# Expert rooms by rank in 53 units, the next layer's adaLN inside the attention, and TensorE weighing two of eight choices

## What is computed

```python
def _trunk_layer(x, mod, layer_idx, p, ctx=None):
    sh1, sc1, g1, sh2, sc2, g2 = jnp.split(mod[:, None, :], 6, axis=-1)
    h = _rmsnorm(x, p['norm_g'][0]) * (1 + sc1) + sh1
    proj = h @ p['w_in']
    ...
    mix = jnp.concatenate([fn_out, a, hg_out], axis=-1) @ p['w_out']
    x = x + g1 * mix
    h2 = _rmsnorm(x, p['norm_g'][1]) * (1 + sc2) + sh2
    x = x + g2 * _moe(h2.reshape(b * l, D_MODEL), p).reshape(b, l, D_MODEL)

def _moe(h, p):
    scores = jax.nn.sigmoid((h @ p['w_router']).astype(jnp.float32))
    ...
    _, eidx = lax.top_k(jnp.where(emask, biased, -jnp.inf), TOP_K)
    w = jnp.take_along_axis(scores, eidx, axis=1)
    w = w / jnp.sum(w, axis=-1, keepdims=True) * ROUTED_SCALE
    gates = jnp.sum(jax.nn.one_hot(eidx, N_EXPERTS, dtype=jnp.float32) * w[..., None], axis=1)
    hg = jnp.einsum('td,edf->tef', h, p['w_gate'])
    hu = jnp.einsum('td,edf->tef', h, p['w_up'])
    act = jax.nn.silu(hg) * hu * gates[:, :, None].astype(h.dtype)
    routed = jnp.einsum('tef,efd->td', act, p['w_down'])
    shared = (jax.nn.silu(h @ p['ws_gate']) * (h @ p['ws_up'])) @ p['ws_down']
    return routed + shared

# mod of layer l: jax.nn.silu(c) @ w_ada[l] + b_ada[l]   (6 x 1024 values; c_ctx for the prompt)
```

## Time and profile before

| | |
|---|---|
| median of 3 runs | 1691.47 us (1687.89 to 1701.95) |
| the profiled execution | 1706.42 us, span 1704.6 us |
| TensorE busy in the span | 1406.1 us (82%) |
| DVE, ACT, POOL busy | 671.4, 408.3 and 256.3 us |
| mean granted TensorE clock | 0.881 of full speed |
| chain that ended last | TensorE 71%, DVE 16%, DMA 6%, issue 4% |

### The profile page before, as it was taken

How to read it: one execution, slowest core, us unless ns; L and a number is a source line. 1 busy time by engine, 2 the same in 40 slices (tenths; PEclk the granted TensorE clock), 3 DMA queues, 4 the chain that set the end, 5 groups by cost and what they waited for, 6 DMA issues and landing times.

```text
span 1704.6 us, 23713 instructions
## 1 busy us (share of the span) xinstructions
PE 1406.1 (82%) x8772; PEld 962.6 (56%) x8772; DVE 671.4 (39%) x1382; ACT 408.3 (24%) x788; POOL 256.3 (15%) x273
## 2 busy tenths in 40 slices
PE   4799687986999999997059996888889999999942
PEld 2598465954555555554028875676655555555521
DVE  4422767153332222222743347633523222222246
ACT  2324425021222222221013344321112122222201
POOL 1000000001322222231010000000023232322200
PEclk9799857977999999999579996699889999999975
DMA  9553202126988888885874412122469888888853
GB/s 319 206 183 118 105 31 109 50 87 233 362 305 317 328 333 324 305 332 181 340 257 173 141 70 99 41 99 99 180 252 358 333 313 307 324 294 298 328 207 154
DMA packets 126098, 378.96 MB, mean 222 GB/s; under 512 B 28224, under 2 KB 33152, under 8 KB 122784
## 3 DMA queue, kind: packets, MB, share of 16 engines
q1 hardware_dynamic: 86976, 291.31, 46.2%
q0 software_dynamic: 35552, 60.97, 10.1%
q10 hardware_dynamic: 3456, 25.17, 3.6%
HBM read 480.36 MB, written 64.75 MB: 320 GB/s over the span
## 4 chain that ended last, share of the span: by engine, by line
PE 71%; DVE 16%; DMA 6%; issue 4%; ACT 2%; SPq 0%; DVEq 0%; ACTq 0%; POOLq 0%
PE bank L1143 25%; PE bank L1158 11%; PE bank L1129 7%; PE bank L1050 5%; PE bank L771 4%; PE bank L772 4%; PE bank L773 4%; DVE aT L1843 4%; DMA ring<-in_w_ada 3%; DVE aT L1580 1%; PE bank L1066 1%; DMA ring<-in_w_in 1%; PE bank L790 1%; PE bank L1114 1%; PE bank L976 1%
## 5 line engine op out<-in xcount | busy, mean ns | idle before, releaser
L1143 PE MATMUL bank<-slab,xT 128*64 128x256 f32 x2112 | 301.5, 396 | 20.6 <-issue 20.5
L1143 PEld LDWEIGHTS bank<-slab,xT 128*64 128x64 f32 x2112 | 180.6, 142 | 104.2 <-issue 38.2
L732 POOL DMA_INDIRECT sums_scratch<-h,row_table x112 | 112.8, 1007 | 538.6 <-PE bank L1129 438.4
L1826 DVE TENSOR_TENSOR work<-work,bank 128x128 f32<-128x128 f32 x112 | 32.3, 288 | 399.1 <-ACT work L1405 399.1
L1143 PE MATMUL bank<-ring,xT 128*64 128x256 f32 x960 | 152.7, 392 | 9.6 <-issue 9.6
L1158 PE MATMUL bank<-slab,work 128*64 128x512 f32 x528 | 147.3, 592 | 1.5 <-DVE work L1832 1.5
L1405 ACT ACTIVATE work<-bank 128x128 f32<-128x128 f32 x112 | 31.1, 278 | 457.5 <-PE bank L1143 457.5
L1815 DVE COPY h<-bank 128x512 f32<-128x512 f32 x112 | 77.5, 692 | 127.0 <-PE bank L1158 127.0
L1143 PEld LDWEIGHTS bank<-ring,xT 128*64 128x64 f32 x960 | 90.1, 140 | 44.8 <-issue 14.8
L1143 PE MATMUL bank<-h_hi_slot,xT 128*64 128x256 f32 x512 | 108.5, 396 | 6.4 <-issue 6.4
L1492 DVE TENSOR_TENSOR w_lo<-ring,w_hi 128x2048 fp32r<-128x2048 f32 x24 | 55.0, 2292 | 122.3 <-ACT w_hi L1229 122.3
(11 more groups left out here) (334 smaller groups left out, 2324.9 us busy)
## 6 DMA issues: line engine op xcount, KB each, us to landing
slab<-in_w_gate SPq DMA_DIRECT2D x112, 512.0 KB
slab<-in_w_up SPq DMA_DIRECT2D x112, 512.0 KB
slab<-in_w_down SPq DMA_DIRECT2D x112, 512.0 KB
ring<-in_w_ada SPq DMA_DIRECT2D x24, 2048.0 KB
ring<-in_w_gate SPq DMA_DIRECT2D x52, 512.0 KB
ring<-in_w_up SPq DMA_DIRECT2D x52, 512.0 KB
ring<-in_w_down SPq DMA_DIRECT2D x52, 512.0 KB
slab<-sums_scratch ACTq DMA_DIRECT2D x24, 1024.0 KB, 11.5
```

Source lines behind the costliest of these rows:

```text
L732: pool.indirect_dma_start(sums_dram, bass.IndirectOffsetOnAxis(ap=row_table[:, u:u + 1], axis=0), y_rows[:, n % 3, :], None, bounds_check= ...
L1143: last = mm(bk[r, 0:2 * P].rearrange("p (k f) -> p k f", k=2), xT[:, n % 2, j, r], w[:, j, :, :], start=(j == 0), stop=(j == NJ - 1))
```

## The change

- Rooms by rank. `windows_of` gives each unit its tiles: ranks 0 to 7 have 128 rows each, now as one tile of 128 columns ("whole", 8 units); ranks 8 to 15 have 96 rows and share their unit with a rank of 56 to 63, which has 32 rows ("mixed", 8 units, tiles 0:64, 64:96 and 96:128); ranks 16 to 47 have 64 rows (16 "pair" units); ranks 48 to 55 have 32 (2 "quad" units of four). With 19 spares there are 53 units and 102 loads, 38 of them conditional.
- The order: turn 0 is pair, whole, pair, mixed, spare, spare; the others pair, whole, spare, pair, mixed, spare; turns 2 and 5 add quad and spare, turn 7 a spare.
- Dispatch: room, place and the first place in the spares of each expert now come from a table by rank (`by_rank`, made once at the start), picked by a one-hot of the rank in three small products ("rooms") behind two tiles of the shared expert's up products, and copied back by DVE.
- adaLN: products 2, 3, 4 stand before the levels and at levels 2 and 4, turned at levels 1 and 3 and after the states. Products 0 and 1 of layer 1 ("ada6", "ada7") are made in the attention of layer 0: product 6 ahead of the first scores, turned at unit 3, product 7 at unit 5, turned at 8. So layer 1 starts with the weights of q and k, loaded as soon as the last expert in the ring is through, and splits w_hi and w_lo of q before its norm. b_ada and norm_g of both layers are loaded at the start.
- Sums: TensorE multiplies two of the eight choices of a tile by diagonal matrices of their gates (`weighed`, 16 products per tile) and adds DVE's sum of the other six by products with the identity (`joined`) in the same bank. DVE spreads the diagonals at unit 9.
- The counting of semaphores is done per layer instead of by formula.

```diff
-NUNITS = 56
-WHOLE = 16
-PAIRED = 24
-NXW = 32
+NUNITS = 53
+BASE_UNITS = 34
+SPARE = NUNITS - BASE_UNITS
+NXW = 2 * SPARE
...
+def windows_of(unit):
+
+    if unit < 8:
+        return [(0, P, unit)]
+    if unit < 16:
+        return [(0, 96, unit), (96, P, unit + 48)]
+    if unit < 32:
+        return [(0, WIN, unit), (WIN, P, unit + 16)]
+    if unit < BASE_UNITS:
+        return [(GROUP * k, GROUP * (k + 1), 48 + 2 * k + unit - 32) for k in range(4)]
+    return [(0, WIN, 64 + unit - BASE_UNITS), (WIN, P, 64 + unit - BASE_UNITS + SPARE)]
...
         for turn in range(8):
-            for kind in ("pair", "whole", "pair", "spare", "pair", "whole", "spare"):
+            kinds = ("pair", "whole", "spare", "pair", "mixed", "spare") if turn > 0 else ("pair", "whole", "pair", "mixed", "spare", "spare")
+            for kind in kinds + {2: ("quad", "spare"), 5: ("quad", "spare"), 7: ("spare",)}.get(turn, ()):
                 u = UNITS_BY_KIND[kind].pop(0)
...
+                for lo, hi, w in windows_of(u):
+                    cuts = [lo, 64, hi] if hi - lo == 96 else [lo, hi]
+                    tiles += [(slice(p, q), len(loads)) for p, q in zip(cuts, cuts[1:])]
+                    loads.append((len(order_of_units), w))
...
             if prev < 0:
-                sp.wait_ge(slots_idle.sem, slots_idle.at(l, 0))
+                if l > 0:
+                    banks.read(sp, "Yb", 0, last_in_ring, f"layer{l - 1}")
+                    banks.read(sp, "XTb", 0, last_x_in_ring, f"layer{l - 1}")
...
-                modulation_product(0)
+                if l == 0:
+                    modulation_product(0)
                 pe.wait_ge(squared.sem, squared.at(l, 1))
                 mean_square("ms1")
...
-                modulation_product(3)
+                modulation_product(2)
 
                 for n in range(NLEV):
                     if n == 1:
+                        modulation_turned(2)
+                    if n == 2:
+                        modulation_product(3)
+                    if n == 3:
                         modulation_turned(3)
+                    if n == 4:
+                        modulation_product(4)
...
+                if l + 1 < DEPTH:
+                    modulation_product(6)
...
+                bk = banks.claim(pe, "rooms")
+                banks.wait_emptied(pe, "ranks")
+                for k in range(3):
+                    last = mm(bk[:, k * E:(k + 1) * E], by_rank[:, k * P:(k + 1) * P], of_rank[0:E, :], start=True, stop=True)
+                banks.filled(last, "rooms")
...
                     for j in range(NJ):
-                        for half in range(2):
-                            r = slice(WIN * half, WIN * (half + 1))
-                            w = expert_slot(n, half)[0][:, 0:2 * D].rearrange("p (k j f) -> p j k f", k=2, j=NJ)
+                        for r, i in tiles_of_unit[n]:
+                            w = load_slot(i)[0][:, 0:2 * D].rearrange("p (k j f) -> p j k f", k=2, j=NJ)
                             last = mm(bk[r, 0:2 * P].rearrange("p (k f) -> p k f", k=2), xT[:, n % 2, j, r], w[:, j, :, :],
                                       start=(j == 0), stop=(j == NJ - 1))
...
+                def weighed(t):
+
+                    m = 4 * t
+                    pe.wait_ge(sums_in_full[m % 6], 16 * (l * 2 + m // 6 + 1))
                     for half in range(2):
                         bk = banks.claim(pe, "yT", 2 * t + half)
                         for j in range(4):
-                            last = tr(bk[:, j * P:(j + 1) * P], y_sum[:, t, 4 * half + j:D:NJ], ident)
+                            for i in range(2):
+                                last = mm(bk[:, j * P:(j + 1) * P], sums_in[:, m % 6, i * D + 4 * half + j:(i + 1) * D:NJ],
+                                          gate_diag[:, 2 * t + i, :], start=(j == 0 and i == 0), stop=False)
+                    last.then_inc(sums_weighed.sem, 1)
```

More of the change, by code:

```diff
@@ L406, in trunk_program @@
-        banks.turn = 0
-        for stage, n in (("ada4", 2), ("oT", NTILE), ("hgT", 2), ("modT4", 2)):
-            banks.plan("layer", stage, n)
-        for stage, n in (("out", NJ), ("ms2", 1), ("ada5", 2), ("router", 1),
-                         ("hr", 2 * NTILE), ("modT5", 2)):
-            banks.plan("layer", stage, n)
-        banks.plan("layer", "sh", 2, [7, 0])
-        banks.plan("layer", "places", 1, [6])
-        banks.plan("layer", "ranks", 1, [7])
-        banks.plan("layer", "ysh", 2 * NTILE, [0, 1, 2, 3, 4, 5])
@@ L524, in trunk_program @@
-        UNITS_BY_KIND = {"whole": list(range(WHOLE)), "pair": list(range(WHOLE, WHOLE + PAIRED)),
-                         "spare": list(range(WHOLE + PAIRED, NUNITS))}
-        order_of_units = []
-        loads, loads_of_unit = [], []
+        for l in range(DEPTH):
+            blocks = []
+            for m in range(2 if l == 0 else 0):
+                blocks += modulation_blocks(l, m)
+            for name, c0 in (("q", Q0), ("k", K0), ("v", V0)):
+                blocks.append((name, [(NJ, 512, 0, in_cols(l, c0, 512))]))
+            blocks.append(("fn+hq", [(NJ, 256, 0, in_cols(l, 0, 256)), (NJ, 256, 2048, in_cols(l, HQ0, 256))]))
+            blocks.append(("hif", [(NJ, 512, 0, in_cols(l, HI0, 512))]))
+            blocks.append(("hbg", [(NJ, 512, 0, in_cols(l, HB0, 512))]))
+            for m in (2, 3, 4) + ((6, 7) if l + 1 < DEPTH else ()):
+                blocks += modulation_blocks(l, m)
+            for half in range(2):
+                blocks.append(("out", [(4, 1024, 0, w_out_v[l][:, 4 * half:4 * half + 4, :])]))
+            blocks += modulation_blocks(l, 5)
+            assert len(blocks) % NSLOT == 0
+            fixed.append(blocks)
@@ new lines, in trunk_program @@
+        landed, fix_sum = [[] for _ in range(DEPTH)], [[0] * NSLOT for _ in range(DEPTH)]
+        for l in range(DEPTH):
+            for b, (_, parts) in enumerate(fixed[l]):
+                fix_sum[l][b % NSLOT] += 16 * len(parts)
+                landed[l].append(fix_sum[l][b % NSLOT])
+        UNITS_BY_KIND = {"whole": list(range(8)), "mixed": list(range(8, 16)), "pair": list(range(16, 32)),
+                         "quad": list(range(32, BASE_UNITS)), "spare": list(range(BASE_UNITS, NUNITS))}
@@ L534, in trunk_program, with slot_before @@
                 order_of_units.append(u)
-        assert sorted(order_of_units) == list(range(NUNITS)) and len(loads) == E + NXW
+        assert all(w < E for _, w in loads[:XSLOT])
+        assert sorted(order_of_units) == list(range(NUNITS)) and sorted(w for _, w in loads) == list(range(E + NXW))
         def slot_uses(s):
             return sum(1 for i in range(len(loads)) if i % XSLOT == s)
-        slot_layer = [fix_sum[r] + 48 * slot_uses(XSLOT - NSLOT + r) for r in range(NSLOT)]
+        def slot_before(l, r):
+            return sum(fix_sum[k][r] + 48 * slot_uses(XSLOT - NSLOT + r) for k in range(l))
@@ new lines, in trunk_program, with reads_to @@
+        last_fill = [{block_of(l, "out", 1): ("out", NJ - 1)} for l in range(DEPTH)]
+        for l in range(DEPTH):
+            for m in range(8):
+                if ("ada%d" % m) in [n for n, _ in fixed[l]]:
+                    last_fill[l][block_of(l, f"ada{m}", 1)] = (f"ada{m}", 1)
+        def reads_to(l, b):
+            return sum(1 for k in range(b) if k not in last_fill[l] and k not in split_blocks[l])
+        reads_before = [sum(reads_to(k, len(fixed[k])) for k in range(l)) for l in range(DEPTH)]
@@ L1132, in up @@
                 def up(n):
-                    for half in range(2):
-                        _, full, level = expert_slot(n, half)
+                    for i in sorted({i for _, i in tiles_of_unit[n]}):
+                        _, full, level = load_slot(i)
                         pe.wait_ge(full, level(l))
@@ L1501, in _ @@
             for l in range(DEPTH):
-                order.enter("layer", l)
                 banks.enter("layer", l)
@@ L1833, in _ @@
                 rows_kept(NUNITS - 1)
-                banks.read(dve, "Yb", 0, NUNITS - 1)
-                dve.sem_inc(slots_idle.sem, 1)
                 def gates_applied(t):
-                    for pair in range(4):
+                    for pair in range(1, 4):
                         m = 4 * t + pair
```

451 lines of the change are left out of this document (241 added, 210 removed).

## The result

The changed kernel takes 1902.99 us (median of 4 runs, 1896.96 to 1916.06) against 1693.8 for the kernel before, measured beside it: a ratio of 1.124, with a 95% interval of 1.117 to 1.132. It is 209 us slower. The forecast was 1848 with a range up to 1885: the direction and the main mechanism came, the size was too small by 55 us, 18 us beyond the range.

What follows compares the result with a forecast made beforehand. The prediction took TensorE as the bound in the expert-unit stages, with holes waiting for loads. Two stages at +174 us and the rest at -16 gave +158, scaled to 157 on the 1691.5 median: 1848 us, range 1700 to 1885.

Steps and rivals of the forecast that it cites:

- the dispatch: Choosing rooms by rank adds a trip from DVE to TensorE and back: +2.5 us per layer, +5, bounds 0 and +10.
- the attention of layer 0: Product 6 ahead of the first scores and product 7 between them lengthen it: +9 us, bounds 0 to 16.
- stalls of 54 us: Unit stage, per layer: units wait for bunched expert loads, mostly at mixed units, quads and following pairs; 18.3 us before.
- colder products of 16.5: Unit stage, per layer: slower products behind holes, 1.1 us for each of seven short holes, 2.2 for four long.
- the third rival: TensorE's waits inside mixed units drop its clock to 1.2 GHz: +40 us, up to 1885; no separate chance given.
- The mixed units: Unit stage: alternating 64- and 32-column tiles run one after another, 7.8 us extra per unit, 62.4 us per layer.
- The rival of sizes side by side: Both tile sizes run together, so mixed units cost nothing extra: +43 us, about 1735, chance 0.20.
- the rule: Unit stage: k expert loads land 2.5 + 5.24k us after the first issue, compared with when the fed unit comes.
- The start of layer 1: Earlier products 0 and 1 and early w_hi, w_lo let q start sooner: -18.7 us, bounds -10 and -20.
- the start of layer 0: q's weights no longer land behind the 2 MB block of ada2: -5 us, bounds 0 to -7.
- the scale of 0.9%: Whole kernel: the profiled 1706.4 us is 0.9% above the median 1691.5, so +158 us is scaled to 157.
- The rival on the other side: Unit stage: mixing is free and weights land faster, at 400 GB/s; stage 378 us, about 1656 in all, chance 0.15.

Runs made afterwards that it cites:

- experiment 1: Changed kernel with all tiles of the mixed units cut to 32 columns: 1795.38 us, ratio 1.062.
- experiment 4: Changed kernel with the order of its 53 units rewritten, one quad first, the other last, a spare behind nearly every two-expert unit: 1802.56 us, ratio 1.065.
- experiment 11: Kernel of experiment 8 with its 56 units in a new order, no run of more than four real loads: 1652.69 us, ratio 0.972.
- experiment 12: Kernel before with only the unit order of experiment 11, no other edit: 1665.45 us, ratio 0.981.
- experiment 3: Changed kernel with the turned rows of modulation 5 put back in PSUM banks 3 and 4: 1894.54 us, ratio 1.118.
- experiment 7: Kernel of experiment 5 with product 7 of the next layer's adaLN moved behind the attention: 1680.86 us, ratio 0.990.
- experiment 5: Changed kernel with the edits of experiment 1, experiment 3 and experiment 4 together: 1688.92 us, ratio 0.996.
- experiment 9: Kernel of experiment 7 with another unit order, the second quad last but one and a spare last: 1696.06 us, ratio 1.001.
- experiment 2: Changed kernel with a mixed unit's up products run first for the 64-column tile, then for both 32-column tiles: 1879.40 us, ratio 1.106.
- experiment 8: Kernel of experiment 7 with the 56 units and order of the kernel before, no mixed or quad units: 1679.62 us, ratio 0.989.

## Where the prediction was right and where it failed

**Which steps failed.** The spans differ by 198.4 us where the forecast had 158, and no single term makes the gap. Two steps were wrong in kind: the dispatch, where only the rooms' own trip was priced (+5, bounds 0 and +10) and the wait that the moved products make in the rotation of banks stood at nothing (measured +18.0); and the attention of layer 0, where idle time of TensorE was taken as room for product 7 (+9 forecast, +14.7 measured). In the unit stage the mechanism was right and the terms too small: stalls of 54 us measured 62.5 and 61.2, colder products of 16.5 measured 21.5. Those two terms had no bounds of their own; the upper end of the range, 1885, was built from the third rival alone, which did not occur as it stood there.

**The mixed units: right.** The earlier trace rows were the nearest rows, and the price taken from them, 7.8 us per unit, was measured at (9.12 - 3.67) + (3.99 - 1.92) = 7.5; 1.14 us for one j came as worked out, and not by luck: the starts of the first products, 450.56, 450.82 and 451.13, lie 0.26 and 0.31 apart, which are the prediction's 0.26 and its 0.22 + 0.09. The rival of sizes side by side, 0.20, did not occur, and experiment 1 shows that the tile size is the cause. "TensorEngine Tiling (Array Packing)" of the Trainium skill, Tiling Modes, Key Properties, was right for a change from 64 to 32 columns: by these runs a change costs 0.13 us, and the larger part, 3.6 of 5.5 us, is that products of the two sizes take their turns one after another. The page "TensorE: Matmul & The Clock Gate" of the Trainium skill, Part 3, holds for tiles of one size (64 products of 32 columns in 3.66 us) and not for two.

**The stalls: mechanism right, 54 us against 62.5 and 61.2.** Experiments 4, 11 and 12 show that the order of the loads makes them. Two kinds of hole were larger. The quads' were 9.7 and 10.2 us in the first stage and not 8.1, for which the prediction shows no working. The last three loads of the first quad are issued in one run; SP's queue has the first and the last of them at

```profile
573.48 0.33 SPq L676 DMA_DIRECT2D ring<-in_w_gate  x1
...
582.03 0.33 SPq L676 DMA_DIRECT2D slab<-in_w_gate  x1
```

By the rule three loads from 573.48 on land at 573.48 + 2.5 + 15.7 = 591.7, and the quad starts at 592.10. So the landing was right to 0.4 us, and the step that was off is the cover: the quad would have started at 592.10 - 9.69 = 582.4, only 8.9 us after that issue. The pairs behind the quads waited 9.0 and 8.5 us and not 7.4. In SP's queue the next unit's load was issued right behind the pair's,

```profile
608.18 0.33 SPq L676 DMA_DIRECT2D ring<-in_w_gate  x1
...
610.53 0.34 SPq L676 DMA_DIRECT2D ring<-in_w_gate  x1
```

and products started at 617.56, 9.4 us after the first issue, where 2.5 + 5.24 gives 7.7. That two loads share the rate is the likely reading; no run isolates it. The other holes came out near the sum and not one by one: before the mixed units 24 and 44 they were 3.8 and 3.6 us and not 1.6, before 10, 16, 30, 36 and 50 together 14.7 and not 18.9. No row shows the rule's 2.5 us alone: with 5.24 us for each load, the quad's three leave 2.9 and the five of unit 9 leave 3.6.

**Colder products: 16.5 against 21.5.** What is left of the stage, 486.1 - 341.9 - 60.2 - 62.5, is 21.5 us. Of these, 17.7 are seen in the up products of the four mixed units, two quads and two pairs that stand behind the long holes. I priced a hole of 4 us ahead of a mixed unit like one ahead of a pair, 1.1 us; four of the eight mixed units took 10.5 to 11.9 us in place of 9.1, up to 2.8 more. The windows of the slowest, its first 5.3 us and the next 6.0, show the granted clock (the column before the last two) at 0.50, the level of 1.2 GHz, and then at 0.92:

```profile
509.70:515.00 5.30, 5.29 (x16) 1.41 (x18) 0.00 (x0) 0.00 (x0) 0.00 (x0) 0.50 0.60 210
515.00:521.00 6.00, 6.00 (x32) 1.62 (x31) 0.00 (x0) 0.00 (x0) 0.00 (x0) 0.92 0.00 0
```

The whole stage: 474.8 forecast, 486.1 and 485.3 measured. Against 387.3 and 391.1 that is +99 and +94, 193 for both, where I had 174 (I had set 387.5 for both layers).

**The dispatch: +5 against +18.0.** This step failed by itself. I priced the rooms' trip (2.5 per layer) and it came at 2.6 and 4.8; but I did not follow the plan of the banks, whose rotation the moved products shift. TensorE's shared products, and behind them the counts per expert, waited for a reduction that DVE does only after its selection: 5.3 us in each layer, by experiment 3. I had asked what is queued behind each new wait, but not which old waits change place when an entry leaves a list that hands out resources in turn.

**The attention of layer 0: +9 against +14.7.** TensorE was idle 6 of 33 us there, and I let the products fall half into that. The chain runs through TensorE, ScalarE and VectorE in turn, and its idle time is not free time: product 7 (3.64 us) with its turning (1.4 in the chain of waits) cost 9 (experiment 7), while 8.5 us of idle time lay just behind. In the changed kernel's timeline the scores twice wait for the work that follows product 7 (L1291 copies its rows, L1558 sums its turned ones):

```profile
270.37 2.13 PE L1035 MATMUL bank<-slab 64*128 64x384 f32 x4 [2.36 <-ACT mod_rows L1291]
...
282.25 1.00 PE L1035 MATMUL bank<-slab 64*128 64x384 f32 x4 [1.64 <-DVE mod L1558]
```

So the banks that product 7 and its turning take from the scores are part of the price. How large a part is not shown, since some of these 4.0 us would have been waited for VectorE anyway.

**Small terms.** The start of layer 1 gave -16.7 of -18.7 (q starts 22.9 us after x is ready, before 39.6); the start of layer 0 -5.8 of -5, counted from its x, which itself is ready 1.2 us later (the room tables stood at 0); the projections -3.2 and -2.8 of -2.7 each. The levels and the scan's output came to +7.8 where +8 stood; the sums and the end -7.8 of -9. Of the 40 us missing between 158 and 198.4, 19 lie in the stages, 13 in the dispatch, 5.7 in the attention and 2 at the start of layer 1.

**From the profile to the median: 15 us.** The forecast stood on the median of 1691.5 from three runs; the median of four is 1693.8, and the scale of 0.9% took only 1 us off the 158. Together this is 4 us: 158 on 1693.8 gives 1852. With the measured 198.4 it gives 1892. The other 11 us no term could have held: the profiled run of before was a long one, 12.6 us above its median (1706.42 to 1693.8), that of the changed kernel lies 1.8 above its own (1904.83), so the spans differ by 11 us less than the medians. The prediction's step of treating such an offset as a factor for the whole has no support in these two.

**What it rested on in the end.** 120 us for two tile sizes (16 units at 7.5) and 87 for the holes (44 and 43) and some 24 more for colder products are the change's price in the two stages, and 39 were won by three units fewer. The rival on the other side, 0.15, needed stalls, cold products and mixing under 53.6 us in a stage; they were 144. But its picture of a 53-unit kernel as fast as the one before was reached with one tile size and another order (experiments 5 and 7). It is not shown what a good order of 53 units could reach in the end: the orders of experiments 5 and 9 came from the same recurrence, and their stages missed it by up to 10 and 13 us. As far as it is shown, 56 units in a good order (1652.69) are ahead of the best 53 (1680.86).

## What to carry to other kernels

Where matmuls of different tile sizes take turns, count each size as a pass of its own, and try all tiles of a unit at the smallest size it needs: here 64 and 32 columns became 32 alone, for 105 us. Where a ring of slots feeds uneven units, write out the issue and the landing of each load against the start of its unit before counting the units: here the order alone was worth 32 us in the old kernel, 100 in the new and 28 in the mended one with 56 units, and three units less were worth nothing beside it. When work is moved out of a rotation of banks, print the new assignment next to the old one: whoever comes later in the list has moved too.

## What the hardware showed that I had not expected

- A change of tile size between 64 and 32 columns costs 0.13 us (experiment 2), and the two sizes take turns: the first product of one starts 0.31 us after the last start of the other, where products of one size start 0.22 us apart, at a granted clock of 1.00.
- 64 products of 32 columns and 256 elements take 3.66 us, 32 of 64 columns 3.67: splitting tiles of 64 columns into 32 costs TensorE nothing here (experiment 1).
- The weights' transfers were not at a limit at the 301 GB/s of the kernel before: with another order 320 GB/s were moved in the same stage (experiment 11), and the 64 loads were ready in 369 us.
- The last scatter before the sums took 8.0 us with a quad last (experiment 7), 2.1 with an empty spare last (experiment 8), and 6.4 with a spare last behind a quad (experiment 9). Layer 0 ends 42.9 to 45.6 us after it has landed, in every kernel with the new sums.
